# A two-layer transformer step on one core: even and odd heads of the first mixer in turn on the upper and lower rows of the matmul array, small products placed among long ones, and the first experts' rows gathered between their first weight blocks

## The chip, the core and the metric

The kernel runs on one core of a Trainium2 chip. A core has TensorE (PE; its weight loads are listed as PEld), VectorE (DVE), ScalarE (ACT), GpSimd (POOL) and a queue engine (SP) that issues the DMAs here. The metric is the device time of one execution in microseconds; the time of the kernel before is the median of three runs.

## The reference, cut to what matters

The program computes a first block and then two layers of a second one, for 256 tokens of width 1024. The change lies in the first block alone. Its mixer has a gated linear attention (GLA) with 4 heads (key width 64, value width 128, both directions, chunks of 64 tokens) and a Hyena branch (two long convolutions); after it come a router and 16 experts that take 32 tokens each.

```python
def _gla_direction(q, k, v, la, s0, with_output):
    kc, vc, lac = _chunk(k), _chunk(v), _chunk(la)
    b = jnp.cumsum(lac, axis=3)
    b_last = b[:, :, :, -1]
    upd = jnp.einsum('bhncd,bhnce->bhnde', kc * jnp.exp(b_last[:, :, :, None] - b), vc)
    ...
    scores = jnp.einsum('bhncd,bhnsd->bhncs', qc * jnp.exp(b - ref), kc * jnp.exp(ref - b))
    ...
    o = (jnp.einsum('bhncs,bhnse->bhnce', scores, vc)
         + jnp.einsum('bhncd,bhnde->bhnce', qc * jnp.exp(b), s_prev))

def _hyena(hp, conv_w, conv_b, filt, bias):
    u = _short_conv(hp, conv_w, conv_b)
    v, x1, x2 = jnp.split(u, 3, axis=-1)
    z = x1 * _bidir_fftconv(v, filt[0, 0], filt[0, 1], bias[0])
    return x2 * _bidir_fftconv(z, filt[1, 0], filt[1, 1], bias[1])

def _ec_moe(h, w_router, w_gate, w_up, w_down):
    ...
    vals, idx = lax.top_k(jnp.swapaxes(aff, 1, 2), cap)
    xs = h[bidx, idx]
    hid = jax.nn.silu(jnp.einsum('becd,edf->becf', xs, w_gate)) * jnp.einsum('becd,edf->becf', xs, w_up)
```

## The kernel before

Each engine runs its own list of instructions, and semaphores join them. For the first mixer the list is a table of steps, `MIX1`: a setup, then four strands (projections and Hyena; GLA of direction 0; GLA of direction 1 with its output; late blocks of the `ada` weights) that `merged` deals out by the cost in `COST` and the share of each strand. The table `AFTER` holds a step back until another has been dealt. All engines walk through `MIX1` in the same order, each doing its own part of a step. So the order of PE, DVE and ACT in the mixer comes from this one table.

The steps that matter here, by the names in the code and the lines of the profile:

- `st(d, s)` (L845), the chunk updates of direction `d` for context (`s` = 1) or latents (0): 16 products with 64 contracted rows and 64 columns of weights. Two loops, the outer one over `odd`, which decides the half of the 128 rows.
- `scr(d, e)` (L855), the scores inside chunks: for the even heads (`e` = 0, rows 0 to 63) and then the odd ones (rows 64 to 127) 4 products each.
- `o_(e)` (L872 and L876), the output of the even and then of the odd heads: products of all 128 rows (values by scores) and of 64 rows (state by queries), four groups of 2 and 4 instructions in a call.
- `osum` (L885): sums of squares of the output, 8 products with one column. ACT squares first (L2675). `ob` turns the result round (L640).
- `ht` (L672), `sp` (L683), `hy` (L635), `ut` (L640), `cv` (L748), `ic` (L635): Hyena's filters, their spectra, its projections (12, in three weight blocks), the transpose before a transform, the transform, and the way back. `sp` and `cv` take four PSUM banks in a row. DVE multiplies the spectra between `cv` and `ic` (L1720 to L1739).
- `ada` (L700): 8 steps with one weight block each, whose sum `mod(1)` (L713) spreads.
- `out` (L635) and `rows`: the output projection, its transposes and the router's products; then softmax (ACT L2731), top 32 of each expert (DVE L1904 to L1913) and a gather of tokens by a product with a 0/1 matrix, `slots(x)` (L635, 16 instructions), in front of the products of experts 4x to 4x+3, `four_experts` (L959).

One product in float32 shows as two matmul records in the trace.

All weights come as blocks of up to 2 MB through a ring of places in SBUF in a fixed order on SP's queue. A block's DMA is issued when the block that had its place before has been read. In the mixer three places are in use; the others lie over the mixer's own buffers. They open when those are done: the first of them waits for `ic(1, 3)`, the next ones also for `o`, and one for the last `out`. Ten blocks fit before the first experts' block must have been read.

```python
                if block_before(i) is not None:
                    q.wait_ge(*at("read", block_before(i)))
                if i == SLOTS.index(4):
                    q.wait_ge(*at("ic", 1, 3))
                if SLOTS[i] in (YE_SLOT, XS_SLOT, HM_SLOT):
                    q.wait_ge(*at("full", "o", 1))
```

Of the kernel before, what the change touches and what calls it, by code (L numbers as in the profile page):

```python
# [117 lines left out]
AFTER = {("hy", 0): ("sp", 1), ("b", 1, 1): ("v", 1, 1), ("o", 0): ("scr", 0, 1)}  # L118
# [265 lines left out]
def rows64(e):  # L384
    return slice(64 * e, 64 * e + 64)
# [5 lines left out]
def program(nc, ring_d, ranked_d, p1_d, p2_d, pf_d, xT_d, cT_d, pos_d, out_d):  # L391
    order, slot_read = [], []
    with contextlib.ExitStack() as ctx:
# [216 lines left out]
        def tensor(g):  # L610
# [224 lines left out]
            def st(d, s):  # L835

                g.wait_ge(*at("kt", d, s))
                g.wait_ge(*at("v", s, 1))
                for odd in range(2):
                    ps, r = fresh("st", d, s, odd), rows64(odd)  # L840
                    for ti in range(2):
                        for hp in range(2):
                            for e in range(2):
                                hd, c = 2 * hp + e, ti * 256 + hp * 128
                                ins = g.matmul(ps[rows64(e), c:c + 128], KT[d][r, ti, hd * 64:(hd + 1) * 64],  # L845
                                               vT[s][r, ti, hd * 128:(hd + 1) * 128], start=True, stop=True)
                    ins.then_inc(*full("st", d, s, odd))

            def scr(d, e):
                r = rows64(e)  # L850
                ps = fresh("scr", d, e)
                g.wait_ge(*at("k2", d))
                for hp in range(2):
                    for ti in range(2):
                        ins = g.matmul(ps[:, (hp * 2 + ti) * 128:(hp * 2 + ti + 1) * 128], KT[d][r, hp, ti * 128:(ti + 1) * 128],  # L855
                                       K1[d][r, hp, ti * 128:(ti + 1) * 128], start=True, stop=True)
                ins.then_inc(*full("scr", d, e))

            def o_(e):
                ps = fresh("o", e)  # L860
# [5 lines left out]
                for hp in range(2):  # L866
                    hd = 2 * hp + e
                    hv, r = slice(hd * 128, (hd + 1) * 128), rows64(e)
                    for ti in range(2):
                        c0 = hp * 256 + ti * 128  # L870
                        for d in range(2):
                            g.matmul(ps[:, c0:c0 + 128], vT[0][:, ti, hv], SCR[d][:, e, hp, ti, :], start=d == 0, stop=False)  # L872
                        for n in (2 * ti, 2 * ti + 1):
                            for d in range(2):
                                o0 = c0 + 64 * (n % 2)
                                ins = g.matmul(ps[:, o0:o0 + 64], SP[r, d, n, hp, :], Q2[d][r, hp, 64 * n:64 * n + 64],  # L876
                                               start=False, stop=n % 2 == 1 and d == 1)
                ins.then_inc(*full("o", e))
# [23 lines left out]
            def out_(b):  # L902
# [46 lines left out]
            def four_experts(ps, key, done, rows_of, ready=None):  # L949

                for part in range(4):
                    w, i = weights(*key, part)
                    wv = w.rearrange("p k (e n) -> p k e n", e=4) if len(w.shape) == 3 else w.rearrange("p (k e n) -> p k e n", k=2, e=4)
                    if ready:
                        g.wait_ge(*at(*ready, part // 2))
# [15 lines left out]
            def slots(x):  # L971
# [3 lines left out]
                g.wait_ge(*at("pm", x > 0))  # L975
                for q in range(2):
# [5 lines left out]
                    ins.then_inc(*full("xs", x, q))  # L982

# [17 lines left out]
            slots(0)  # L1001
# [18 lines left out]
            for x in range(4):  # L1020
                for half in range(2):
                    for mat in range(2):
                        ps = fresh("gu", x, half, mat)
                        four_experts(ps, (("w_gate", "w_up")[mat], x, half), ("gu", x, half, mat),
                                     lambda kk, e: XS[x][:, kk, 32 * e:32 * e + 32], ("xs", x))
# [551 lines left out]
        def vector(v):  # L1577
# [344 lines left out]

            def slots(x):
# [8 lines left out]
            slots(0)  # L1932
# [587 lines left out]
        def scalar(s):  # L2520
# [147 lines left out]
            def o_(e):  # L2668
                full("o", e)
                s.activation(OS.rearrange("p (h e) t -> p h e t", e=2)[:, :, e, :], bank("o", e).rearrange("p (h t) -> p h t", h=2), ACT.Copy) \  # L2670
                    .then_inc(*out("o", e))
# [27 lines left out]
            def normed(ti):  # L2699
                s.activation(HT[:, ti, :], HT[:, ti, :], ACT.Copy, bias=0.0, scale=RS1[:, ti:ti + 1]).then_inc(*out("hn", ti))  # L2700

# [24 lines left out]
            s.activation(STAT[:, 62:63], EPS5, ACT.Exp, bias=0.0, scale=1.0).then_inc(*out())  # L2726
# [3 lines left out]
            s.wait_ge(*at("lsub"))  # L2730
            s.activation(AE, AE, ACT.Exp, bias=0.0, scale=1.0).then_inc(*out("aexp"))  # L2731
            normed(1)
            slots(0)
# [656 lines left out]
```

## Time and profile before

| what | value |
|---|---|
| median of three runs | 1692.89 us (1688.23, 1694.29, 1692.89) |
| the profiled execution | 1685.1 us |
| its span in the trace | 1683.2 us |
| PE busy | 1423.9 us (85%) |
| PEld busy | 796.6 us (47%) |
| DVE busy | 509.1 us (30%) |
| ACT busy | 314.7 us (19%) |
| moved by DMA | 492.62 MB, mean 293 GB/s |
| granted clock of TensorE, mean | 0.921 of 2.4 GHz |

The span is the time between the first and the last record; 1.9 us of the execution lie around it. The shares are averages over stages with different limits: the first mixer ends at about 286 us, the first block's experts at about 745 us, and the two layers of the second block follow. A granted clock of 0.50 in a stretch is the lower of the two levels, 1.2 GHz, and 1.00 the upper one, 2.4 GHz.

### The profile page before, as it was taken

The numbers are of one execution on the slowest core, as the hardware profiler recorded it, in microseconds if no ns is written. First come the engines' busy times: TensorE is split into PE (matmuls) and PEld (weight loads), VectorE is DVE, ScalarE is ACT, GpSimd is POOL, SyncE is SP. The second block draws the span as 40 slices with busy tenths as digits, with TensorE's granted clock in tenths as the row PEclk, the third lists the DMA queues.
The fourth block names the chain that finished last, engine by engine and source line by source line (L and its number), as shares of the span: only waits on it lengthen the run. The fifth ranks groups of instructions, "written<-read, shape, count | busy, mean of one in ns | idle before, by whom it ended". The sixth has DMA issues, their size and how long they took to land.

```text
span 1683.2 us, 19028 instructions
## 1 busy us (share of the span) xinstructions
PE 1423.9 (85%) x7528; PEld 796.6 (47%) x7528; DVE 509.1 (30%) x1140; ACT 314.7 (19%) x659; POOL 0.2 (0%) x4
## 2 busy tenths in 40 slices
PE   6999998765766656579999899987899998999877
PEld 3665777321221211146768643432467677434323
DVE  5125362200111100014674422221336644222213
ACT  2422111100000000012322312210222223122102
POOL 0000000000000000000000000000000000000000
PEclk9999799888887878789999899999999999999989
DMA  9465219999999999991521389999715123799994
GB/s 383 167 228 200 100 50 390 382 428 428 427 428 428 428 428 427 426 415 53 200 100 51 150 338 412 412 417 411 322 50 200 64 87 150 311 415 408 416 413 161
DMA packets 56386, 492.62 MB, mean 293 GB/s; under 512 B 6240, under 2 KB 6624, under 8 KB 25952
## 3 DMA queue, kind: packets, MB, share of 16 engines
q1 hardware_dynamic: 56144, 491.15, 71.4%
q8 instruction: 66, 1.08, 0.3%
q14 instruction: 32, 0.26, 0.0%
q10 hardware_dynamic: 144, 0.13, 0.0%
HBM read 490.21 MB, written 1.05 MB: 292 GB/s over the span
## 4 chain that ended last, share of the span: by engine, by line
PE 60%; DMA 25%; DVE 6%; SPq 6%; issue 2%; ACT 1%; DVEq 0%; ACTq 0%
DMA A<-ring_d 21%; PE PS L635 20%; PE PS L1455 7%; SPq L3059 6%; PE PS L1484 4%; PE PS L959 4%; DMA A<-ranked_d 4%; PE PS L1319 3%; PE PS L640 3%; PE PS L1435 2%; PE PS L1501 2%; PE PS L1308 1%; PE PS L1145 1%; PE PS L1272 1%; PE PS L700 1%
## 5 line engine op out<-in xcount | busy, mean ns | idle before, releaser
L635 PE MATMUL PS<-A 128*128 128x256 f32 (+6 forms) x1720 | 413.7, 399 | 5.0 <-DMA A<-ring_d 2.7
L959 PE MATMUL PS<-A 128*32 128x512 f32 x1536 | 236.6, 753 | 143.4 <-DMA A<-ring_d 143.1
L635 PEld LDWEIGHTS PS<-A 128*128 128x128 f32 (+1 forms) x1720 | 308.5, 197 | 100.8 <-issue 58.4
L1455 PE MATMUL PS<-A 128*64 128x512 f32 (+1 forms) x1024 | 197.5, 635 | 23.7 <-DMA A<-ranked_d 23.6
L959 PEld LDWEIGHTS PS<-A 128*32 128x32 f32 x1536 | 52.2, 124 | 317.9 <-issue 239.7
L1455 PEld LDWEIGHTS PS<-A 128*64 128x64 f32 (+1 forms) x1024 | 58.5, 131 | 142.9 <-issue 141.0
L1975 DVE TENSOR_TENSOR A<-A,PS 128x512 f32<-128x512 f32 x8 | 5.5, 688 | 331.1 <-PE PS L959 331.1
L1484 PE MATMUL PS<-A 128*64 128x512 f32 (+1 forms) x512 | 94.9, 597 | 0.7 <-issue 0.7
L640 PE MATMUL PS<-A 128*128 128x128 f32 (+1 forms) x444 | 69.5, 289 | 29.2 <-DVE A L1975 7.1
L640 PEld LDWEIGHTS PS<-A 128*128 128x128 f32 (+1 forms) x444 | 53.5, 148 | 69.0 <-issue 39.2
L2426 DVE TENSOR_TENSOR A<-A,PS 128x256 f32<-128x256 f32 x26 | 11.0, 423 | 214.5 <-ACT A L2964 214.5
L1319 PE MATMUL PS<-A 128*128 128x256 f32 x256 | 58.3, 383 | 2.3 <-DVE A L2240 1.2
L1484 PEld LDWEIGHTS PS<-A 128*64 128x64 f32 (+1 forms) x512 | 27.1, 126 | 64.6 <-issue 63.3
L1501 PE MATMUL PS<-A 128*128 128x512 f32 x104 | 52.4, 628 | 5.2 <-issue 5.2
L1319 PEld LDWEIGHTS PS<-A 128*128 128x128 f32 x256 | 47.7, 190 | 10.5 <-issue 3.0
L2964 ACT ACTIVATE A<-PS 128x256 f32<-128x256 f32 x26 | 10.0, 386 | 224.9 <-PE PS L1455 224.9
L1435 PE MATMUL PS<-A 128*128 128x256 f32 (+1 forms) x256 | 49.3, 343 | 0.0
L2432 DVE COPY A<-PS 128x512 f32<-128x512 f32 x26 | 18.0, 692 | 102.0 <-PE PS L1484 102.0
L1435 PEld LDWEIGHTS PS<-A 128*128 128x128 f32 x256 | 41.0, 190 | 15.6 <-issue 12.0
L2069 DVE TENSOR_TENSOR A<-PS,A 128x512 f32<-128x512 f32 (+1 forms) x24 | 16.5, 688 | 63.2 <-PE PS L1145 63.2
L2878 ACT ACTIVATE A<-A 128x128 f32<-128x128 f32 (+1 forms) x48 | 21.2, 443 | 75.4 <-DVE A L2202 75.4
L2421 DVE TENSOR_SCALAR A<-PS,A 128x256 f32<-128x256 f32 (+1 forms) x64 | 28.6, 489 | 18.3 <-PE PS L1435 17.6
(352 smaller groups left out, 1259.6 us busy)
## 6 DMA issues: line engine op xcount, KB each, us to landing
A<-ring_d SPq DMA_DIRECT2D x156, 2048.0 KB, 23.3
A<-ranked_d SPq DMA_DIRECT2D x72, 1024.0 KB, 16.4
A<-ranked_d SPq DMA_DIRECT2D x144, 512.0 KB, 15.3
A<-ring_d SPq DMA_DIRECT2D x2, 1312.0 KB, 21.7
A<-ring_d SPq DMA_DIRECT2D x2, 1280.0 KB, 21.9
A<-p_d SPq DMA_DIRECT2D x1, 1232.0 KB, 21.9
A<-xT_d SPq DMA_DIRECT2D x1, 1024.0 KB, 5.6
A<-cT_d SPq DMA_DIRECT2D x1, 1024.0 KB, 12.0
```

The source lines that it names most:

```text
L635: ins = g.matmul(out, l, r, start=n == 0, stop=n == len(pairs) - 1)
L640: return g.transpose(out, in_, ident[0:k, 0:k])
L959: ins = g.matmul(ps[32 * e:32 * e + 32, :], rows_of(kk, e), wv[:, kk % 2, e, :], start=kk == 0, stop=kk == 7)
L1319: ins = g.matmul(bank("wo", l, b)[:, j * 256:(j + 1) * 256], w[:, k, c:c + 128], O[:, k, :], start=k == 0 and j == 0, stop=k == 7, skip_gr ...
L1435: ins = g.matmul(ps[:, c:c + w], XGT[:, x, d * 128:(d + 1) * 128], px, start=True, stop=True)
L1455: ins = g.matmul(ps[m * s:m * s + m, :], XS2[u % 2][:, kk, c:c + m], wv[:, kk % nk, s, :], start=kk == 0, stop=kk == 7)
L1484: ins = g.matmul(ps[m * s:m * s + m, :], HD[n % 2][:, f, m * s:m * s + m], wd[f][:, s, half * 512:(half + 1) * 512], start=f == 0, stop=f ...
L1501: ins = g.matmul(PS[:, b, :], QT[p % 2], YE2[p % 2][:, half * 512:(half + 1) * 512], start=n == 0, stop=last)
L2421: ins = v.tensor_scalar(XS2[u % 2][:, d, 0:w], bank("xs2", l, u, part, 1)[:, j * 256:j * 256 + w], gain, bias, ALU.mult, ALU.add)
L2432: v.tensor_copy(YE2[p % 2][:, 512:1024], bank("ye2", l, p, 1)).then_inc(*out("ye2", l, p, 1))
L2878: ins = s.activation(p, p, ACT.Exp, bias=ST[:, i, c:c + 1], scale=1.0, accum_out=ST[:, i, 4 + c:5 + c])
L3059: q.dma_start(RING[x][:, s * n:(s + 1) * n], src).then_inc(*land(f"ring{x}", *(("landed", i) if s == len(of) - 1 else ())))
```

## The change

The change does four things.

1. In `st`, `scr` and `o_` the loop over the two halves of the rows becomes the inner one, so that products on rows 0 to 63 and rows 64 to 127 follow each other, into two PSUM banks. `scr(d, 0)` does both halves and `scr(d, 1)` nothing on PE. `o_(hp)` now does one pair of heads, even and odd, and keeps both banks from the first call to the second; ACT copies both after the second.
2. Eight entries of `AFTER` instead of three, of which these change the order:

```diff
-AFTER = {("hy", 0): ("sp", 1), ("b", 1, 1): ("v", 1, 1), ("o", 0): ("scr", 0, 1)}
+AFTER = {("hy", 0): ("sp", 1), ("b", 1, 1): ("v", 1, 1), ("o", 0): ("hy", 3), ("o", 1): ("cv", 0), ("osum",): ("hy", 7), ("ob", 0): ("ic", 0, 3),
+         ("mod", 1): ("ic", 0, 3), ("sp", 0): ("ada", 9), ("sp", 1): ("ada", 10)}
```

3. The first `out` product no longer waits for `ic(1, 3)` as a whole: the first seven of its eight parts wait for `ic(1, 2)`, the last for `ic(1, 3)`. On ACT the load of the exponential's table and the softmax's exponential move ahead of the last copy of `rows` and of both `normed` steps.
4. The gather for experts 0 to 3 is cut in four, `first_slots(q)`: two parts stand ahead of the first weight block of `w_gate`, the third ahead of the second block and the fourth ahead of the third. Each block waits for its own part alone. ACT takes over parts 0 and 2 from PSUM and DVE parts 1 and 3.

```diff
             def st(d, s):
+                ps = [fresh("st", d, s, odd) for odd in range(2)]
                 g.wait_ge(*at("kt", d, s))
                 g.wait_ge(*at("v", s, 1))
-                for odd in range(2):
-                    ps, r = fresh("st", d, s, odd), rows64(odd)
-                    for ti in range(2):
-                        for hp in range(2):
-                            for e in range(2):
+                for ti in range(2):
+                    for hp in range(2):
+                        for e in range(2):
+                            for odd in range(2):
...
             def scr(d, e):
-                r = rows64(e)
-                ps = fresh("scr", d, e)
+                if e:
+                    return
+                ps = [fresh("scr", d, x) for x in range(2)]
                 g.wait_ge(*at("k2", d))
                 for hp in range(2):
                     for ti in range(2):
+                        for x in range(2):
+                            r = rows64(x)
+                            ins = g.matmul(ps[x][:, (hp * 2 + ti) * 128:(hp * 2 + ti + 1) * 128], KT[d][r, hp, ti * 128:(ti + 1) * 128],
+                                           K1[d][r, hp, ti * 128:(ti + 1) * 128], start=True, stop=True)
...
+            def o_(hp):
+                for x in range(2):
+                    if hp == 0:
+                        fresh("o", x, hold=True)
+                ps = [bank("o", x) for x in range(2)]
...
+                for ti in range(2):
+                    c0 = hp * 256 + ti * 128
+                    for x in range(2):
+                        hd = 2 * hp + x
                         for d in range(2):
+                            g.matmul(ps[x][:, c0:c0 + 128], vT[0][:, ti, hd * 128:(hd + 1) * 128], SCR[d][:, x, hp, ti, :], start=d == 0, stop=False)
+                    for n in (2 * ti, 2 * ti + 1):
+                        for d in range(2):
+                            o0 = c0 + 64 * (n % 2)
+                            for x in range(2):
+                                r = rows64(x)
+                                ins = g.matmul(ps[x][:, o0:o0 + 64], SP[r, d, n, hp, :], Q2[d][r, hp, 64 * n:64 * n + 64],
                                                start=False, stop=n % 2 == 1 and d == 1)
...
                 g.wait_ge(*at("mix", 1))
-                g.wait_ge(*at("ic", 1, 3))
-                for j in range(2):
-                    c = (b % 2) * 256 + j * 128
-                    ins = group(ps[:, j * 256:(j + 1) * 256], [(hold["outw"][:, k, c:c + 128], T[:, k, :]) for k in range(8)])
+                for k0, k1 in ((0, 7), (7, 8)) if b == 0 else ((0, 8),):
+                    g.wait_ge(*at("ic", 1, k1 - 5))
...
                 for part in range(4):
+                    for q in ahead[part]:
+                        first_slots(q)
                     w, i = weights(*key, part)
...
+            def first_slots(q):
+                g.wait_ge(*at("hn", 0))
+                g.wait_ge(*at("hn", 1))
+                g.wait_ge(*at("pm", False))
+                ps = fresh("xs", 0, q)
+                for j in range(2):
+                    c = (2 * q + j) * 128
+                    ins = group(ps[:, j * 128:(j + 1) * 128], [(HT[:, ti, c:c + 128], places_of(ti, 0, 4).rearrange("p e j -> p (e j)"))
+                                                               for ti in range(2)])
+                ins.then_inc(*full("xs", 0, q))
...
+                                     ((), (), (), ()) if x or half or mat else ((0, 1), (2,), (3,), ()))
...
                     s.activation(MS1, MS1, ACT.Sqrt, bias=EPS6, scale=1.0).then_inc(*out("hstd"))
+                    s.activation(STAT[:, 63:64], EPS5, ACT.Exp, bias=0.0, scale=1.0).then_inc(*out())
+                    s.wait_ge(*at("lsub"))
+                    s.activation(AE, AE, ACT.Exp, bias=0.0, scale=1.0).then_inc(*out("aexp"))
```

**PE around the filters' spectra.** L672 is `ht`, L855 `scr`, L845 `st`, L683 `sp`, L700 `ada`, L635 `hy`. Before:

```order
L672 MATMUL PS<-A 128x512 x5
L855 MATMUL PS<-A 128x128 x4
L672 MATMUL PS<-A 128x512
L845 MATMUL PS<-A 64x128 x16
L672 MATMUL PS<-A 128x512
L855 MATMUL PS<-A 128x128 x4
L672 MATMUL PS<-A 128x512
L683 MATMUL PS<-A 128x512 x4
L700 MATMUL PS<-A 32x512 x8
L683 MATMUL PS<-A 128x512 x4
L635 MATMUL PS<-A 128x256 x16
```

After, with the lines of the changed kernel (`ht` L673, `scr` L862, `st` L847, `sp` L684, `ada` L701, `hy` L636):

```order
L673 MATMUL PS<-A 128x512 x5
L862 MATMUL PS<-A 128x128 x8
L673 MATMUL PS<-A 128x512
L847 MATMUL PS<-A 64x128 x16
L673 MATMUL PS<-A 128x512 x2
L701 MATMUL PS<-A 32x512 x8
L684 MATMUL PS<-A 128x512 x4
L701 MATMUL PS<-A 32x512 x8
L684 MATMUL PS<-A 128x512 x4
L862 MATMUL PS<-A 128x128 x8
L636 MATMUL PS<-A 128x256 x24
```

An `ada` step has moved in front of the first `sp`, another stands between the two, and the scores of direction 1 follow the second `sp` in one piece.

**PE around the output of GLA and the first transform.** L635 is `hy`, L855 `scr`, L872 and L876 `o_`, L640 `ut`, L748 `cv`, L700 `ada`. Before:

```order
L700 MATMUL PS<-A 32x512 x8
L635 MATMUL PS<-A 128x256 x8
L855 MATMUL PS<-A 128x128 x4
L635 MATMUL PS<-A 128x256 x8
L855 MATMUL PS<-A 128x128 x4
L872 MATMUL PS<-A 128x128 x2
L876 MATMUL PS<-A 128x64 x4
...
L640 MATMUL PS<-A 128x128 x8
L748 MATMUL PS<-A 128x512 x4
L700 MATMUL PS<-A 32x512 x8
L872 MATMUL PS<-A 128x128 x2
```

After (`hy` L636, `o_` L883 and L889, `ut` L641, `cv` L749, `osum` L900):

```order
L701 MATMUL PS<-A 32x512 x8
L636 MATMUL PS<-A 128x256 x8
L883 MATMUL PS<-A 128x128 x4
L889 MATMUL PS<-A 128x64 x8
...
L641 MATMUL PS<-A 128x128 x8
L749 MATMUL PS<-A 128x512 x4
L883 MATMUL PS<-A 128x128 x4
L889 MATMUL PS<-A 128x64 x8
...
L636 MATMUL PS<-A 128x256 x32
L900 MATMUL PS<-A 128x1 x8
```

The output's first half now follows the whole of `hy(3)` with nothing of `scr` between them, its second half follows `cv(0)` directly, and all four of the next `hy` stand ahead of `osum`. In each half the groups are twice as long and half as many.

**PE at the first experts.** L640 is the last transpose of the routing, L635 the gather, L959 the experts' products. Before:

```order
L640 MATMUL PS<-A 128x16 x2
L635 MATMUL PS<-A 128x128 x16
L959 MATMUL PS<-A 32x512 x64
L640 MATMUL PS<-A 128x128 x4
L635 MATMUL PS<-A 128x36 x8
```

After (L641, L636 and L980):

```order
L641 MATMUL PS<-A 128x16 x2
L636 MATMUL PS<-A 128x128 x8
L980 MATMUL PS<-A 32x512 x8
L636 MATMUL PS<-A 128x128 x4
L980 MATMUL PS<-A 32x512 x8
L636 MATMUL PS<-A 128x128 x4
L980 MATMUL PS<-A 32x512 x48
```

The first block of eight products stands behind 8 instead of 16 instructions of the gather.

## Rows read from the trace of the kernel before

**Rows 1.** DMA and engines by stretch: length, busy times, clock, DMA share, GB/s.

```profile
257.00:304.00 47.00, 35.22 (x187) 31.39 (x187) 14.07 (x46) 6.36 (x10) 0.00 (x0) 0.86 1.00 426
304.00:314.00 10.00, 10.00 (x94) 4.50 (x97) 1.37 (x4) 3.39 (x6) 0.00 (x0) 0.98 0.66 245
340.00:740.00 400.00, 251.86 (x1552) 82.48 (x1553) 32.78 (x82) 24.38 (x48) 0.00 (x0) 0.81 1.01 428
```

**Rows 2.** SP's waits from 250 to 300 us, and its first issue after 300 us.

```profile
SPq L3100 <- DVE A L1837: 32.5, 1, 32.5
...
L3100 SPq DMA_DIRECT2D A<-ring_d x1: 336/336/336, 308.1 to 308.1; - x1
DMA to landing us min/median/max: 9.0/9.0/9.0
```

**Rows 3.** DVE from the end of cv(1) to ic(1, 3), first and last instruction.

```profile
234.67 1.22 DVE L1720 TENSOR_TENSOR A<-PS,A 128x1024 f32<-128x1024 f32 x1 [7.51 <-PE PS L748]
...
254.67 0.28 DVE L1837 TENSOR_TENSOR A<-A 128x128 f32<-128x128 f32 x1
```

**Rows 4.** The chain that ended last: start, length, work. Small products of the mixer.

```profile
99.06 1.52 PE PS L845 x32
...
133.34 1.09 PE PS L855 x8
...
192.34 0.64 PE PS L872 x4
192.98 1.03 PE PS L876 x8
```

**Rows 5.** The same chain: the two stretches from ut to the end of cv.

```profile
182.67 1.92 PE PS L640 x8
...
185.35 5.13 PE PS L748 x8
...
229.28 5.36 PE PS L748 x8
```

**Rows 6.** PE in order of time: start, length, work, idle before and its releaser.

```profile
141.35 3.67 PE L683 MATMUL PS<-A 128*128 128x512 f32 x8 [1.16 <-DVE A L1644]
...
170.81 0.82 PE L872 MATMUL PS<-A 128*128 128x128 f32 x4 [1.39 <-DVE A L1817]
...
204.57 2.83 PE L885 MATMUL PS<-A 128*128 128x1 f32 x16 [1.90 <-ACT A L2675]
...
227.30 1.20 PE L640 MATMUL PS<-A 128*128 128x128 f32 x8 [1.67 <-DVE A L1747]
```

**Rows 7.** Busy times and granted clock by stretch around o_(0) and behind osum.

```profile
170.80:188.00 17.20, 16.41 (x59) 13.18 (x60) 0.00 (x0) 1.79 (x3) 0.00 (x0) 0.51 0.24 104
206.00:208.00 2.00, 2.00 (x9) 1.91 (x10) 0.20 (x1) 0.27 (x1) 0.00 (x0) 0.50 0.00 0
```

**Rows 8.** PE in the second block: score products on one row half (first), on both (second).

```profile
862.30 0.93 PE L1270 MATMUL PS<-A 64*128 64x128 f32 x6
863.07 1.46 PE L1272 MATMUL PS<-A 64*128 64x256 f32 x6
...
874.26 0.49 PE L1270 MATMUL PS<-A 64*128 64x128 f32 x4
874.58 0.60 PE L1272 MATMUL PS<-A 64*128 64x256 f32 x4
```

**Rows 9.** ACT in order of time: last copy of rows, table load, normed(0), the exponential.

```profile
288.96 0.58 ACT L2688 ACTIVATE A<-PS 128x512 f32<-128x512 f32 x1
289.55 1.28 ACT L2726 ACT_TABLE_LOAD   x1
...
291.14 1.15 ACT L2700 ACTIVATE A<-A 128x1024 f32<-128x1024 f32 x1
292.20 0.21 ACT L2731 ACTIVATE A<-A 128x32 f32<-128x32 f32 x1
```

**Rows 10.** PE in order of time: the gather for the first experts.

```profile
300.64 5.58 PE L635 MATMUL PS<-A 128*128 128x128 f32 x32 [1.01 <-DVE A L1919]
```

More of the change, by code:

```diff
@@ L909, in out_ @@
                 g.wait_ge(*at("mix", 1))
-                g.wait_ge(*at("ic", 1, 3))
-                for j in range(2):
-                    c = (b % 2) * 256 + j * 128
-                    ins = group(ps[:, j * 256:(j + 1) * 256], [(hold["outw"][:, k, c:c + 128], T[:, k, :]) for k in range(8)])
+                for k0, k1 in ((0, 7), (7, 8)) if b == 0 else ((0, 8),):
+                    g.wait_ge(*at("ic", 1, k1 - 5))
+                    for j in range(2):
+                        c = (b % 2) * 256 + j * 128
+                        for k in range(k0, k1):
+                            ins = g.matmul(ps[:, j * 256:(j + 1) * 256], hold["outw"][:, k, c:c + 128], T[:, k, :],
+                                           start=k == 0 and j == 0, stop=k == 7, skip_group_check=True)
                 ins.then_inc(*full("out", b))
@@ L954, in four_experts @@
                     if ready:
-                        g.wait_ge(*at(*ready, part // 2))
+                        g.wait_ge(*at(*ready, part // 2 if ready[1] else part))
                     arrived(i)
@@ L1921, in places, with first_slots @@
                 ins.then_inc(*out(*key))
+            def first_slots():
+                for q in (1, 3):
+                    full("xs", 0, q)
+                    for j in range(2):
+                        d = 2 * q + j
+                        ins = v.tensor_scalar(XS[0][:, d, :], bank("xs", 0, q)[:, j * 128:(j + 1) * 128], MA[:, 4, d:d + 1],
+                                              MA[:, 5, d:d + 1], ALU.mult, ALU.add)
+                    ins.then_inc(*out("xs", 0, q))
             def slots(x):
@@ L2666, in qk, with o_ @@
                 s.activation(Q2[d], BB[d], ACT.Exp, bias=0.0, scale=1.0).then_inc(*out("q2", d))
[L2668 to L2671, printed above, removed]
+            def o_(hp):
+                if hp == 0:
+                    return
+                for e in range(2):
+                    full("o", e)
+                    s.activation(OS.rearrange("p (h e) t -> p h e t", e=2)[:, :, e, :], bank("o", e).rearrange("p (h t) -> p h t", h=2), ACT.Copy) \
+                        .then_inc(*out("o", e))
             def osum():
@@ L2700, in normed, with first_slots @@
                 s.activation(HT[:, ti, :], HT[:, ti, :], ACT.Copy, bias=0.0, scale=RS1[:, ti:ti + 1]).then_inc(*out("hn", ti))
+            def first_slots():
+                for q in (0, 2):
+                    full("xs", 0, q)
+                    for j in range(2):
+                        d = 2 * q + j
+                        ins = s.activation(XS[0][:, d, :], bank("xs", 0, q)[:, j * 128:(j + 1) * 128], ACT.Identity,
+                                           bias=MA[:, 5, d:d + 1], scale=MA[:, 4, d:d + 1])
+                    ins.then_inc(*out("xs", 0, q))
             def slots(x):
@@ L2729, in scalar @@
             normed(0)
-            s.wait_ge(*at("lsub"))
-            s.activation(AE, AE, ACT.Exp, bias=0.0, scale=1.0).then_inc(*out("aexp"))
             normed(1)
-            slots(0)
+            first_slots()
             for x in range(4):
```

39 lines of the change are left out of this document (14 added, 25 removed).

## The prediction

> **What bounds the kernel now.** I read the DMA by stretch first. From 257 to 304 us the weights flow at 426 GB/s, from 304 to 314 at 245, from 340 to 740 at 428 again, while PE works for only 252 of those 400 us [rows 1]. So the first block's experts are bound by their weights, and their end stands at a fixed distance from the start of that flow. What matters is when the flow starts and whether it has a hole. Its start is in SP's waits: the longest, 32.5 us, ends with DVE's L1837, in the step of `ic(1, 3)`, which opens the fourth place of the ring [rows 2]. That instruction closes 20.0 us of DVE's work without a gap, from 234.67 to 254.67, which starts when PE ends `cv(1)` [rows 3]. So the flow starts 20.0 us after `cv(1)`, and this distance isn't touched. The hole follows from the ring: ten blocks fit, then SP waits until the first experts' block has been read, issues at 308.1, and that block lands 9.0 us later [rows 2]. Its price is 10 us at 245 instead of 428 GB/s, 4.3 us [rows 1].
>
> Ahead of `cv(1)` PE is busy but for three places, which the waits in order of time show: 1.16, 1.39 and 1.67 us for DVE, and besides these 1.90 us for ACT [rows 6]. The granted clock tells the rest. It is 0.51 over the 17.2 us behind the wait of 1.39, the lower level nearly throughout, and 0.50 behind `osum` [rows 7].
>
> Behind the first experts nothing is changed, so I carry the shift to the end at its full size.
>
> **The change part by part.** First the shift of `cv(1)`'s end.
>
> *Row halves in turn.* The nearest rows are the score products of the second block. On one row half 6 records take 0.77 us from start to start, 128 ns each; on both halves in turn 4 take 0.32, 80 ns each; the longer form falls from 1.46/6 = 243 ns to 0.60/4 = 150 [rows 8]. Both ratios are 0.62. `scr` takes 1.09 a call, `o_`'s part of 64 rows 1.03 a group of eight records at the upper clock, `st` 1.52 [rows 4]. With 0.62, four `scr` save 4 x 0.41 = 1.65 us and eight groups of `o_` 8 x 0.39 = 3.1 us. The 128-row part of `o_` keeps its 0.64. `st` already takes only 1.52/32 = 48 ns a record, since its column halves are in turn; I take a third instead of 0.38, 0.5 us for each of four calls, 2.0 us. Bounds: nothing for all three (if the halves don't overlap), and half of each, 2.2 + 4.1 + 3.0 = 9.3 us instead of 6.75.
>
> The Trainium skill, TensorEngine Tiling (Array Packing), section Theoretical Speedup, gives up to 2x for a small dimension of 64 or less; by it these three would save the 9.3 us. The rows on the score products stop at 0.62, and I go by them.
>
> *Waits.* An `ada` step in front of the first `sp` takes 1.86 us (from 190.48, the end of `cv(0)`, to 192.34 [rows 4, 5]) and covers the 1.16 us for DVE. What is late next there is DVE's own list, but it ends its last `ht` about when PE ends that step, so I count the whole 1.16. The 1.39 us before `o_(0)` were for the masks of `scr(1, 1)`; these scores now lie three `hy` and an `ada` earlier: gone. The 1.67 us before `ut(1, 0)` are for DVE's `ic(0, 3)`; `ob` and `mod(1)` now stand between: gone. Sum 4.2 us, bounds 2 and 4.2. The 1.90 us before `osum` stay: ACT squares at its own place in the list, now behind `hy(7)` instead of `hy(4)`, so PE waits for one copy and the square exactly as now. I count nothing.
>
> *Clock.* The 17.2 us at the lower level began with the 1.39 us of idle time. Without it I expect the upper level there. `o_(0)` took 182.67 - 170.81 = 11.86 us; at the upper one the same work takes 4 x (0.64 + 1.03) = 6.68 [rows 4 to 6], 5.2 less. `ut(0)` with its wait took 2.68, `ut(1)` 1.98: 0.7 less. `cv(0)` took 5.13 against 3.67 for `sp`, which has the same form: 1.4 less [rows 5, 6]. Sum 7.3. `cv(1)` took 5.36 behind the wait of 1.67 [rows 5, 6]; without that wait 3.67, 1.7 less. Behind `osum` the wait stays, and I leave the lower clock with it. Sum 9.0 us. Bounds: nothing (if the small products hold the clock down by themselves), and 9.0 + 3 (if `osum`, too, keeps the upper level).
>
> *Sum of the mixer.* 6.75 + 4.2 + 9.0 = 19.9 us: `cv(1)`, and with it the start of the flow, comes 19.9 us earlier. DMAs of the mixer: the blocks of `ada` steps 9, 10 and `hy` go through three places in nearly the same order, and PE waits for none of them in this stretch today. I count nothing; a late block would cost up to 9 us, the landing time above.
>
> *The hole.* It closes as far as the first experts' block is read earlier relative to the flow. On ACT the exponential no longer stands behind the last copy (0.58) and `normed(0)` (1.15) [rows 9]: about 1.6 earlier, and DVE's routing follows it directly. The gather of 16 instructions took 5.58 us; only half of it now stands ahead of the block: 2.8 earlier [rows 10]. But the block comes into the stretch in which PE has just been idle and the clock is low: its 1.86 us (the form of an `ada` step) become up to 3.5, 1.6 lost. Net 2.8 us of the 4.3; bounds 1.2 and 4.3. The split of `out` would add to this and I count it at nothing, since the hole isn't deeper. The two other parts of the gather hide behind the flow, as PE works 63% of it.
>
> *Total.* 19.9 + 2.8 = 22.7 us. The profiled execution took 1685.1 us (span 1683.2), so it would take 1662.4. The median of the three runs is 1692.9, 7.8 above it; I take the same gain from that: **1670 us**. Three runs that lie 6 us apart can hardly tell less than 0.5%, 8.5 us, from no change.
>
> **The rivals.**
>
> *The clock falls at `o_(0)` anyway.* The output's first half and `ut` are small products for 6 us, and then PE waits for ACT's copy. For it: `o_(0)` stayed at the lower level to its end, though PE was busy for 16.4 of the 17.2 us [rows 7]. Against: `o_(1)`, the same products, ran at 0.64 and 1.03 all through [rows 4]. It takes back the 7.3: 1677 us. Chance 0.22.
>
> *The halves don't overlap in `st`, `scr` and `o_`,* since their weights, not their columns, take the time. Against it stand the score products, whose weights are as wide. It takes 6.75: 1677 us. Chance 0.10.
>
> *`osum` keeps the upper clock and the halves come nearer to 2x.* 3 + 2.5 + 1.5 for the hole: 1663 us. Chance 0.10.
>
> *The flow doesn't follow the mixer.* If another condition sets the issue of the first blocks, or a late `ada` or `hy` block takes the place of PE's waits, only the hole and a few us are left: 1684 to 1690 us. SP's wait names L1837 alone. Chance 0.08.
>
> *Slower: each switch between row halves empties the array.* A product then costs its whole way through the array. No row shows that price; the longer score product's pitch on one half, 243 ns [rows 8], is the nearest for a small product that isn't overlapped. At 0.24 us a record instead of 0.048 in `st` (128 records), 0.136 in `scr` (32) and 0.129 in `o_` (64), that is 25 + 3 + 7 = 35 us more than today; against the remaining gain of 16 us the kernel would be 19 us slower: 1712 us. It decides from 0.11 us more a record: 224 x 0.11 = 25 us eats the 16 and the measurement's 8.5. The pitch of 80 ns on alternating halves speaks against it. Chance 0.04.
>
> The Trainium skill, TensorEngine Tiling (Array Packing), section Key Properties, says that a change of the tiling mode, not of the tile, drains TensorE; by that rule halves in turn cost no drain, and the longer groups of `o_` halve its changes between 128 and 64 rows, a gain.
>
> **How the numbers follow.** My own case has 0.46, and between 1665 and 1675 us. The rivals to the fast side reach 1663, the two middle ones 1677, together 1679 to 1683 if both come. The range 1661 to 1682 leaves out some 2 in 10: the flow that doesn't follow, the slow rival, and the tails. Faster by over 0.5% (below 1684.4): 0.46 + 0.22 + 0.10 + 0.10 and a little of the fourth rival, 0.89. Within 0.5%: 0.07. Slower: 0.04.
>
> **What would show it.** PE's waits before `sp(0)`, `o_(0)` and `ut(1, 0)` gone, that before `osum` still near 1.9. Granted clock 1.00 from `o_(0)` to `cv(0)`, and `cv` at 3.7 us twice. Groups of 16 records in `o_` near 1.3 us instead of 2 x 1.03. SP's long wait ends near 235 us, again 20 us behind `cv(1)`. From 50 us behind it the DMA rate dips less than to 245 GB/s over ten us. PE's last expert product of the first block comes 23 us earlier, and no more is lost or won behind it. The prediction fails if PE's idle time only moves, if the clock falls again at a thin stretch, or if a wait for a DMA appears in the mixer.

## The result, and the profile after

The changed kernel takes 1662.36 us (median of 4 runs, 1661.39 to 1666.04); the kernel before, beside it, 1690.56 us (4 runs). The ratio is 0.9851, 95% interval 0.9821 to 0.988. In a second series it took 1662.15 us (6 runs, 1659.62 to 1666.87) against 1687.19, ratio 0.9858 (0.9835 to 0.988). Forecast were 1670 us and a range of 1661 to 1682.

The head of the page of the changed kernel, and its group of the first experts' products:

```profile
span 1659.6 us, 19035 instructions
...
PE 1409.5 (85%) x7528; PEld 781.9 (47%) x7528; DVE 509.7 (31%) x1140; ACT 314.5 (19%) x659; POOL 0.2 (0%) x4
...
L980 PE MATMUL PS<-A 128*32 128x512 f32 x1536 | 242.5, 769 | 138.2 <-DMA A<-ring_d 137.8
```

The span is 23.6 us shorter, and the experts' products still wait for the ring's blocks. The chain that ended last, from the changed kernel's scores to the DVE work behind `cv(1)` (start, length, work; L862 is `scr`, L883 and L889 `o_`, L641 `ut`, L749 `cv`, L636 `hy`):

```profile
132.99 1.09 PE PS L862 x16
...
167.55 0.89 PE PS L883 x8
168.44 1.04 PE PS L889 x16
...
171.61 0.69 PE PS L641 x4
...
173.55 3.67 PE PS L749 x8
...
181.33 0.59 ACT A L2716
...
182.05 14.07 PE PS L636 x64
...
208.71 3.69 PE PS L749 x8
212.42 1.24 DVE A L1754
```

Sixteen records of the scores take as long as eight did in [rows 4], and so do sixteen of the 64-row part of `o_`: 1.04 against 1.03. The eight records of the 128-row part take 0.89, and 1.09 in the second group of a call, where twice four took 1.28. Both `cv` take 3.7 us, against 5.13 and 5.36 in [rows 5]. `cv(1)` ends at 212.40 instead of 234.64, 22.2 us earlier. This trace had also started worse. The same `ada` step, ahead of the first instruction that was edited, before and after:

```profile
68.01 1.92 PE L700 MATMUL PS<-A 128*32 128x512 f32 x16
```

```profile
69.13 1.93 PE L701 MATMUL PS<-A 128*32 128x512 f32 x16
```

It is 1.1 us late there; from 20 to 40 us the granted clock was 0.81 against 0.95. Counted from this step, `cv(1)` moved by 23.4 us. PE's waits from the filters' spectra to `osum`, in order of time:

```profile
140.56 3.67 PE L684 MATMUL PS<-A 128*128 128x512 f32 x8 [0.61 <-DVE A L1678]
...
182.05 14.05 PE L636 MATMUL PS<-A 128*128 128x256 f32 x64 [0.77 <-ACT A L2716]
198.00 1.92 PE L900 MATMUL PS<-A 128*128 128x1 f32 x16 [1.90 <-ACT A L2721]
```

Of the waits in [rows 6] the second and the last are gone, the first has shrunk to 0.61, the one for ACT's square is where it was, and one is new: `hy(4)` waits 0.77 us for ACT's copy of `o_`. Engines and clock by stretch (columns as in [rows 7]) around `o_(0)` to `cv(0)`, behind `osum`, and over 65.5 us from the start of the weight flow; under it the same stretch of the kernel before.

```profile
167.40:177.00 9.60, 8.81 (x65) 6.42 (x64) 0.97 (x2) 2.67 (x4) 0.00 (x0) 1.00 0.86 365
198.00:206.00 8.00, 8.00 (x58) 8.00 (x58) 3.53 (x9) 1.42 (x2) 0.00 (x0) 0.79 0.56 231
232.50:298.00 65.50, 54.55 (x340) 38.90 (x339) 16.43 (x53) 9.85 (x16) 0.00 (x0) 0.90 0.99 410
```

```profile
254.70:320.00 65.30, 53.40 (x340) 39.45 (x340) 15.69 (x52) 9.75 (x16) 0.00 (x0) 0.90 0.94 389
```

The clock is at its upper level, 2.4 GHz, from `o_(0)` to `cv(0)`, and for part of the time behind `osum` at the lower one. The flow moves 410 GB/s on average instead of 389: against the full 428 that leaves 2.8 us of hole instead of 5.9 (65.5 x 18/428, 65.3 x 39/428). Of either, 1.7 us lie in the first 49 us, which flow at 413 GB/s. SP's wait for `ic(1, 3)`, and its first issue behind the ten blocks, as in [rows 2]; then PE at the gather and the first block, as in [rows 10]:

```profile
SPq L3155 <- DVE A L1871: 36.3, 1, 36.3
...
L3155 SPq DMA_DIRECT2D A<-ring_d x1: 337/337/337, 282.6 to 282.6; - x1
...
DMA to landing us min/median/max: 9.2/9.2/9.2
```

```profile
268.39 0.59 PE L641 MATMUL PS<-A 128*16 128x128 f32 x2 [3.57 <-DVE A L1932]
...
275.82 3.75 PE L636 MATMUL PS<-A 128*128 128x128 f32 x16 [1.01 <-DVE A L1953]
279.50 3.00 PE L980 MATMUL PS<-A 128*32 128x512 f32 x16
```

The issue came 25.5 us earlier (308.1 to 282.6), 3.3 us more than the flow's start. The first block took 3.00 us in place of 1.9, at the lower clock, and half the gather took 3.75.

Behind the first block the distance between the two traces isn't constant. First row of PE's products of the second block, and the last row of PE, before and after:

```profile
752.14 17.43 PE L635 MATMUL PS<-A 128*128 128x256 f32 x80
...
1675.28 2.58 PE L640 MATMUL PS<-A 128*128 128x128 f32 x16 [3.14 <-ACT A L2786]
```

```profile
724.05 17.43 PE L636 MATMUL PS<-A 128*128 128x256 f32 x80
...
1650.80 3.43 PE L641 MATMUL PS<-A 128*128 128x128 f32 x16 [3.15 <-ACT A L2841]
```

28.1 us at the start of the second block, 24.5 at the last transposes, which then take 0.85 us longer. At the last sums of squares of the first block it was 26.7 (741.87 and 715.20). I come back to this.

### The profile page after: what moved, and what is told of

Read it like the earlier page. It is cut to its first block, busy times and chain, and to the rows that moved or that the text cites. A ratio compares the mean times of both kernels' runs of the same rounds, so it can differ in the third digit from the quotient of the medians.

```text
span 1659.6 us, 19035 instructions
## 1 busy us (share of the span) xinstructions
PE 1409.5 (85%) x7528; PEld 781.9 (47%) x7528; DVE 509.7 (31%) x1140; ACT 314.5 (19%) x659; POOL 0.2 (0%) x4
## 4 chain that ended last, share of the span: by engine, by line
PE 61%; DMA 25%; DVE 5%; SPq 5%; issue 2%; ACT 1%; DVEq 0%; ACTq 0%
DMA A<-ring_d 21%; PE PS L636 19%; PE PS L1489 8%; SPq L3114 5%; PE PS L1518 4%; PE PS L980 4%; DMA A<-ranked_d 4%; PE PS L1353 3%; PE PS L641 3%; PE PS L1469 3%; PE PS L1535 2%; PE PS L930 2%; PE PS L1342 1%; PE PS L1179 1%; PE PS L1306 1%
## 5 line engine op out<-in xcount | busy, mean ns | idle before, releaser
L636 PE MATMUL PS<-A 128*128 128x256 f32 (+6 forms) x1592 | 383.1, 398 | 4.5 <-DMA A<-ring_d 2.6
L980 PE MATMUL PS<-A 128*32 128x512 f32 x1536 | 242.5, 769 | 138.2 <-DMA A<-ring_d 137.8
L636 PEld LDWEIGHTS PS<-A 128*128 128x128 f32 (+1 forms) x1592 | 283.0, 196 | 97.8 <-issue 60.0
L980 PEld LDWEIGHTS PS<-A 128*32 128x32 f32 x1536 | 53.0, 126 | 316.1 <-issue 244.6
L641 PE MATMUL PS<-A 128*128 128x128 f32 (+1 forms) x444 | 69.3, 289 | 25.9 <-DVE A L2018 7.1
L641 PEld LDWEIGHTS PS<-A 128*128 128x128 f32 (+1 forms) x444 | 54.1, 150 | 64.8 <-issue 32.9
## 6 DMA issues: line engine op xcount, KB each, us to landing
A<-ring_d SPq DMA_DIRECT2D x156, 2048.0 KB, 23.4
```

The costliest lines, as they stand in the source:

```text
L636: ins = g.matmul(out, l, r, start=n == 0, stop=n == len(pairs) - 1)
L641: return g.transpose(out, in_, ident[0:k, 0:k])
L980: ins = g.matmul(ps[32 * e:32 * e + 32, :], rows_of(kk, e), wv[:, kk % 2, e, :], start=kk == 0, stop=kk == 7)
```

## The experiments

My theory: the mixer's end sets the start of the flow, and it moved by three parts, idle time with the slow clock behind it, row halves that overlap, and, behind it, the hole. Rivals: small products hold the clock down by themselves; the halves gain only by fewer changes of the array; the end of the mixer isn't what binds. Times are medians; "before" is the kernel before on the same chip, 1690.13 us (17 runs) for e1 to e4 and 1687.19 us (11 runs) for the rest. The changed kernel itself was not timed beside e1 to e4, so e2 and e4 are set against its ten runs in the two other series, 1659.6 to 1666.9 us.

**e1, the order alone.** The kernel before with the new table.

```diff
-AFTER = {("hy", 0): ("sp", 1), ("b", 1, 1): ("v", 1, 1), ("o", 0): ("scr", 0, 1)}
+AFTER = {("hy", 0): ("sp", 1), ("b", 1, 1): ("v", 1, 1), ("o", 0): ("hy", 3), ("o", 1): ("cv", 0), ("osum",): ("hy", 7), ("ob", 0): ("ic", 0, 3),
+         ("mod", 1): ("ic", 0, 3), ("sp", 0): ("ada", 9), ("sp", 1): ("ada", 10)}
```

> The kernel before with the new table AFTER alone: the order of the mixer's steps, no row halves in turn, no change to out, softmax or the first gather. Theory (the wait ahead of o(0) brings the clock down, and the order removes it): the end of cv(1) comes 13 to 15 us earlier than 234.64, granted clock 1.00 from o(0) to cv(0), time 14 us below the kernel before. Rival (small products of 64 rows one half at a time hold the clock down by themselves, and only the halves in turn keep it up): clock 0.50 from o(0) to cv(0) as before, gain 4 to 6 us.

1676.46 us (6 runs), ratio 0.9937 (0.9913 to 0.9961). PE in order of time at `o_(0)` and `cv(0)` (L873, L877, L749), and the clock over that stretch:

```profile
169.99 0.61 PE L873 MATMUL PS<-A 128*128 128x128 f32 x4
170.53 1.10 PE L877 MATMUL PS<-A 64*128 64x64 f32 x8
...
178.59 3.67 PE L749 MATMUL PS<-A 128*128 128x512 f32 x8 [0.79 <-ACT A L2609]
```

```profile
170.00:182.10 12.10, 11.31 (x65) 8.49 (x64) 0.97 (x2) 3.27 (x5) 0.00 (x0) 1.00 0.69 292
```

No wait stands before `o_(0)`, and the clock is 1.00 although the halves still come one after the other. `cv(1)` ended 14 us earlier (217.01 + 3.67 = 220.7). The rival that needs the halves for the clock falls. The median moved by 13.7 us, the ratio of all runs by 11 (7 to 15).

**e2, the halves apart.** The changed kernel, the loop over halves outermost in `st` and `scr`, and in `o_`:

```diff
-                    for n in (2 * ti, 2 * ti + 1):
-                        for d in range(2):
-                            o0 = c0 + 64 * (n % 2)
-                            for x in range(2):
+                    for x in range(2):
+                        for n in (2 * ti, 2 * ti + 1):
+                            for d in range(2):
+                                o0 = c0 + 64 * (n % 2)
```

> The changed kernel with the two row halves one after the other again inside each group of st, scr and o_; groups, banks and order stay. Theory (the halves overlap): a group of 16 records of o_ takes 2.06 us instead of 1.04, scr 2.2 instead of 1.1, st 1.54 instead of 1.04; 4 + 2 + 2 us, so 8 us slower than the changed kernel. Rival (the gain came from fewer changes between 128 and 64 rows): within 1 us of the changed kernel.

1670.62 us (6 runs), ratio 0.9888 (0.9868 to 0.9907): 8 us above the changed kernel by the medians, as forecast, and 5 to 6 by the ratios; all six runs, from 1667.35, lie above its ten. But the rows aren't those of the forecast. The chain of e2:

```profile
138.10 1.64 PE PS L862 x16
140.79 1.55 PE PS L847 x32
...
174.19 0.89 PE PS L883 x8
175.08 1.53 PE PS L889 x16
```

A group of 16 in `o_` takes 1.53, between the 2.06 of two groups of eight before and the 1.04 of halves in turn; `scr` takes 1.64, between 2.18 and 1.09. So both theories hold a half: joining two groups took off 0.5 us, putting the halves in turn another 0.5. `st` had its groups joined before, and takes 1.55 as then. In this trace the halves apart account for 4 x 0.5 + 2 x 0.55 + 4 x 0.5 = 5.1 us. `cv(1)` ended 9.7 us later than in the trace of the changed kernel (222.1 against 212.4), and the rest of this isn't theirs: e2's trace was 3.6 us late by 72 us already, ahead of the first instruction that was edited, where the same products ran at a lower clock and one wait for a DMA was 0.9 us longer, and behind `osum` the lower clock cost 1.6 us more.

**e3, the tail alone.** The changed kernel with the mixer of before; what stays are the split `out`, the early exponential and the gather in parts.

```diff
-AFTER = {("hy", 0): ("sp", 1), ("b", 1, 1): ("v", 1, 1), ("o", 0): ("hy", 3), ("o", 1): ("cv", 0), ("osum",): ("hy", 7), ("ob", 0): ("ic", 0, 3),
-         ("mod", 1): ("ic", 0, 3), ("sp", 0): ("ada", 9), ("sp", 1): ("ada", 10)}
+AFTER = {("hy", 0): ("sp", 1), ("b", 1, 1): ("v", 1, 1), ("o", 0): ("scr", 0, 1)}
...
-                ps = [fresh("st", d, s, odd) for odd in range(2)]
```

> The changed kernel with the mixer's table, st, scr and o_ of before: only the split out, the early exponential and the gather in four parts are left. Theory (the hole in the weight flow closes by about 3 us): the flow starts at 254.7 as before, time 3 us below the kernel before. Rival (the earlier gather only makes PE wait for the flow): no difference.

1683.04 us (12 runs, 1674.24 to 1689.65), ratio 0.997 (0.9953 to 0.9987), so 5 us (2 to 8) below before by the ratio and 7 by the medians, where I expected 3. Its profiled run is the fastest of the twelve, and shows what I hadn't expected. PE in order of time at `o_(0)` (L872, L876) and `cv(0)` (L748), and the clock:

```profile
170.30 0.68 PE L872 MATMUL PS<-A 128*128 128x128 f32 x4 [1.39 <-DVE A L1836]
170.91 1.10 PE L876 MATMUL PS<-A 64*128 64x64 f32 x8
...
178.97 3.67 PE L748 MATMUL PS<-A 128*128 128x512 f32 x8 [0.79 <-ACT A L2636]
```

```profile
170.30:188.00 17.70, 16.91 (x106) 11.99 (x107) 5.21 (x6) 3.30 (x5) 0.00 (x0) 1.00 0.38 143
```

The mixer is that of before, the wait of 1.39 us is there, and the clock stays at 1.00. In [rows 7] the same stretch was at 0.51. So the wait doesn't always bring the clock down, and what a fall costs can be read off two traces of one mixer: `cv(1)` ended 8 us earlier here (226.8 against 234.64), 7.3 of them from the end of the wait to the end of `cv(0)` (190.48 - 170.81 = 19.7 against 182.64 - 170.30 = 12.3).

How often the fall comes, the times tell roughly. My estimate for the profiled execution of before without it is 1685.1 - 7.3 = 1677.8 us. The fastest of the 32 timed runs of before took 1682.9, and of the twelve of e3 only the profiled one is under 1680. So it is likely the rule in this order of steps, and its absence the exception; no other run's trace shows it.

**e4, the wait put back.** The changed kernel with `scr(1)` directly ahead of `o_(0)`.

```diff
-("o", 0): ("hy", 3), ("o", 1): ("cv", 0)
+("scr", 1, 0): ("hy", 3), ("o", 0): ("hy", 3), ("ut", 0, 0): ("o", 0), ("o", 1): ("cv", 0)
```

> The changed kernel with scr(1) directly ahead of o(0), behind hy(3), so that o(0) waits for DVE's masks again. Theory (that wait brings the clock down): a wait of 1 to 2 us, then 0.50 granted until cv(0) is half through; 1.5 us of wait and 5 to 6 us of slow clock, 7 us slower than the changed kernel. Rival (a wait costs only itself): 1.5 us slower.

1670.17 us (6 runs), ratio 0.9883 (0.986 to 0.9905), 8 us above the changed kernel by the medians and 4 to 5 by the ratios; five of the six runs lie above its ten. PE in order of time:

```profile
170.20 1.13 PE L883 MATMUL PS<-A 128*128 128x128 f32 x8 [1.99 <-DVE A L1851]
171.25 1.24 PE L889 MATMUL PS<-A 64*128 64x64 f32 x16
172.42 2.07 PE L883 MATMUL PS<-A 128*128 128x128 f32 x8
174.43 1.97 PE L889 MATMUL PS<-A 64*128 64x64 f32 x16
...
179.09 5.28 PE L749 MATMUL PS<-A 128*128 128x512 f32 x8 [0.78 <-ACT A L2651]
```

The wait is 1.99 us, and 2 us behind its end the products take twice as long, until `cv(0)` is half through. From the start of `o_(0)` to the end of `cv(0)` it is 14.2 us instead of 9.8, so the slow clock cost 4.3 us, less than the 5 to 6 expected. `cv(1)` ends 8.8 us later than in the changed kernel; the rest is the wait, another of 0.81 us for ACT ahead of `hy(3)` that the edit brought, and 1.6 us more of slow clock behind `osum`. A wait that costs only itself is refuted for this run.

**a1, the changed kernel again.** No edit.

> The changed kernel itself, to have its time on the same chip as the three others: 1662 us if the chip is like the first, its end of cv(1) within 1 us of 212.4.

1662.15 us, the figures above; `cv(1)` ended at 212.3.

**e7, the gather in one piece.**

```diff
-                    for q in ahead[part]:
-                        first_slots(q)
...
             ins.then_inc(*full("post"))
+            slots(0)
```

(In the kernel the list `ahead` is emptied, and ACT and DVE call `slots(0)` too.)

> The changed kernel with the gather for experts 0 to 3 in one piece again (16 instructions ahead of the first block). Theory (the gather's half ahead of the first block sets when the ring's fourth place is free, and so the hole in the flow): the first block is read 1.5 to 2.8 us later, the rate over the ten us around it falls, time 2 us above the changed kernel. Rival (the hole was closed by the earlier exponential alone): no difference.

1665.24 us (6 runs), ratio 0.9866 (0.9846 to 0.9886), against 0.9858 (0.9835 to 0.988) for a1: the medians are 3.1 us apart, the intervals overlap. Its flow by stretch, 65.3 us from its start:

```profile
234.60:299.90 65.30, 54.34 (x353) 40.36 (x352) 16.47 (x54) 10.34 (x17) 0.00 (x0) 0.90 0.97 404
```

404 GB/s lie between the 410 of the changed kernel and the 389 of before: a hole of 3.7 us against 2.8 and 5.9. So in these traces the gather in parts closes 0.9 us of the hole, and the other 2.2 of the 3.1 come from the exponential and the split of `out`. I had given the gather 2.8 - 1.6 = 1.2, and the exponential 1.6.

The 0.9 depends on the clock at the first block. In the changed kernel and a1 it took 3.00 and 2.93 us; in e2, e3, e4, e8 and e9, with the same gather, 1.92 to 1.98, and there such a stretch flowed at 415 or 416 GB/s. Against those the parts close 1.7 to 1.8 us. By time alone the gain of the gather isn't shown: the trace of e7 is 2.3 us late at the end of `cv(1)`, where nothing was edited.

**e8, longer groups in `o_`.** All the 128-row products of a call first, then its 64-row ones.

```diff
                         for d in range(2):
-                            g.matmul(ps[x][:, c0:c0 + 128], vT[0][:, ti, hd * 128:(hd + 1) * 128], SCR[d][:, x, hp, ti, :], start=d == 0, stop=False)
+                            g.matmul(ps[x][:, c0:c0 + 128], vT[0][:, ti, hd * 128:(hd + 1) * 128], SCR[d][:, x, hp, ti, :],
+                                     start=d == 0 and ti == 0, stop=False, skip_group_check=True)
+                for ti in range(2):
+                    c0 = hp * 256 + ti * 128
```

> The changed kernel with the two groups of each call of o_ joined: 8 products of 128 rows, then 16 of 64 rows, so that the array changes between the two half as often. Theory (each change costs some tenths of a us, which is why eight 128-row records took 1.0 instead of 1.28 in the changed kernel): 0.2 to 0.3 us less in each call, 0.5 us in all, not to be told from the changed kernel by time. Rival (no cost in a change): the same length of a call, 4.2 us.

1662.71 us (6 runs), ratio 0.9864 (0.9841 to 0.9886): not to be told from a1. PE in order of time, `o_(0)` whole, then `ut`:

```profile
167.39 1.95 PE L883 MATMUL PS<-A 128*128 128x128 f32 x16
169.26 2.00 PE L892 MATMUL PS<-A 64*128 64x64 f32 x32
171.20 1.23 PE L641 MATMUL PS<-A 128*128 128x128 f32 x8
```

A call takes 3.81 us (171.20 - 167.39) where it took 4.15 in a1 (171.43 - 167.28). Two changes between 128 and 64 rows fewer save 0.34 us, 0.17 each.

**e9, what is left of the waits.** e8, ACT's square right behind its copies, and the banks of `o` held until `hy(4)` has its own:

```diff
+                settle()
+                s.activation(OQ, OS, ACT.Square, bias=0.0, scale=1.0).then_inc(*out("oq"))
 
             def osum():
-                settle()
-                s.activation(OQ, OS, ACT.Square, bias=0.0, scale=1.0).then_inc(*out("oq"))
...
+                if m == 4:
+                    banks.release("o", 0)
+                    banks.release("o", 1)
```

> The changed kernel with three further edits: ACT squares the output of GLA right behind its two copies instead of behind hy(7); the two banks of o are released only when hy(4) has its bank, so that hy(4) doesn't wait for ACT's copies; the groups of e8. Theory: the 1.90 us ahead of osum and the 0.77 us ahead of hy(4) go, the clock stays up behind osum (1.6 us), and with 0.5 us of the groups cv(1) ends 4 to 5 us earlier, time 1658 us. Rival (another wait takes their place, as osum's result is needed no earlier): less than 1.5 us.

1659.34 us (6 runs, 1657.02 to 1666.09), ratio 0.9842 (0.9818 to 0.9866). PE in order of time (L636 `hy`, L905 `osum`, L752 `cv(1)`), and the clock:

```profile
179.52 14.08 PE L636 MATMUL PS<-A 128*128 128x256 f32 x64
193.44 1.84 PE L905 MATMUL PS<-A 128*128 128x1 f32 x16
...
203.05 3.67 PE L752 MATMUL PS<-A 128*128 128x512 f32 x8 [1.39 <-DVE A L1702]
```

```profile
193.00:207.00 14.00, 12.61 (x86) 10.43 (x85) 8.13 (x21) 4.22 (x6) 0.00 (x0) 1.00 0.41 152
```

Both waits are gone and the clock stays up behind `osum`; `cv(1)` waits 1.39 instead of 0.79, now for DVE, and ends 5.6 us earlier than in a1 (206.7 against 212.3), of which 0.9 was there at `o_(0)` already, ahead of the first edit (166.38 against 167.28). No fall of the clock follows this wait of 1.39 us either. The median is 2.8 us below a1's, but the intervals of the ratios overlap, so by time alone it isn't shown to be faster than the changed kernel.

## Why the prediction was right

Its frame held: the flow of weights starts 20 us behind `cv(1)` (232.44 - 212.42 = 20.0 again), and the first block's end moves with the flow. e1 shows it from the other side, with the mixer alone 14 us shorter. The sum for the mixer was 19.9 us, measured 22.2, or 23.4 counted from 68 us. Term by term, from the two traces:

| term | forecast | measured |
|---|---|---|
| `st` | 2.0 | 1.9 (four times 1.52 to 1.04) |
| `scr` | 1.65 | 2.2 (two pairs, 2.18 to 1.09) |
| `o_`, 64 rows | 3.1 | 4.1 (four pairs, 2.06 to 1.04) |
| `o_`, 128 rows | 0 | 1.2 (5.12 to 3.96) |
| waits | 4.2 | 2.8 (0.55, 1.39 and 1.67 gone, 0.77 new) |
| clock, `o_(0)` to `cv(0)` | 7.3 | 7.3 (11.86, 2.68, 5.13 to the upper level's times) |
| clock at `cv(1)` | 1.7 | 1.7 |
| clock around `osum` | 0 | about 1.8 (in these two traces) |
| hole | 2.8 | 3.1 |

The measured column adds to 23.0 for the mixer, 0.4 short of the 23.4. The 1.8 around `osum` is partly luck: e1, e2, e4 and e7 have the same steps from `osum` on, and in them the lower clock lasted longer, so that the way from `osum` to the transposes behind took 8.7 us against 7.1 in the changed kernel, a1 and e8.

*Where it was off.* The step "Both ratios are 0.62" was mis-sized for `scr` and `o_`: against before the measured ratio is 0.5. The 0.62 came from rows of the second block in which groups of 6 and of 4 records are compared, so that nothing was joined, and in e2 the halves in turn alone give 1.04/1.53 = 0.68 and 1.09/1.64 = 0.66, close to it; the rest is the joining, which I hadn't priced, although the order rows showed it. Here the bound of up to 2x for 64 rows came out nearer, which the Trainium skill gives (TensorEngine Tiling (Array Packing), section Theoretical Speedup) and which the prediction set against its rows, but half of it for a reason that the section doesn't name. The 128-row part gained by it as well. By e8 a change between 128 and 64 rows costs 0.17 us; the Trainium skill says in the section Key Properties of that page that a change of the mode drains TensorE, and gives no figure.

*The waits.* The sum "I count the whole 1.16" was wrong by half: DVE's own list was late, as the text said it might be, and 0.61 remained. The new wait of 0.77 had no term: both banks of `o_` are freed by ACT only after the second call, and `hy(4)` takes the first of them. That is a wait in the place of another, small enough.

*The clock.* Its size was right. Its cause was put too simply. "The 17.2 us at the lower level began with the 1.39 us of idle time" is what the trace shows; that without the wait the clock stays up was borne out in e1 and the changed kernel, and e4 brought the fall back with the wait. But e3 shows the wait without the fall, and in e9 a wait as long before `cv(1)` had none behind it. So the change takes away the occasion of a fall that cost 7.3 us, which by the times came in most runs with this order of steps and in one trace was absent. The rival "the clock falls at `o_(0)` anyway" came in none of the seven traces that have that order and no wait there (the changed kernel twice, e1, e2, e7, e8, e9).

*The hole.* 3.1 us by the rates, close to the 2.8. Inside it the gather was worth 0.9, not 1.2, and `out` and the exponential 2.2. Both terms of the gather were too large. The half ahead of the block took 3.7 us (279.50 - 275.82), since it is the half at the lower clock (granted 0.50 there), where the whole took 5.5 in e7 (283.57 - 278.04): 1.8 saved, not 2.8. The block at the lower clock took 3.0 us, which gave back 1.1, not 1.6. "The split of `out` would add to this and I count it at nothing" left out a term: DVE's last addition for `out` (L1844 before, L1878 after) comes 0.9 us earlier relative to the flow, and the softmax's sums (L1894, L1928) 1.7 more, which is the exponential's 1.6. Neither was run apart.

*The rivals.* The fast one, halves near 2x and the upper clock behind `osum`, had 1663 us and a chance of 0.10. Its first half came, its second for a part of the stretch, and the kernel lies at its figure: the likeliest case named the right mechanisms and took `scr`, `o_` and the clock behind `osum` too small. The two middle rivals together would give 1670 + 7.3 + 6.75 = 1684 us, not 1679 to 1683; nothing hangs on it, as neither came.

*The time.* From the profiled execution the forecast was 1662.4 us, measured 1661.5. From the median it was 1670, measured 1662.4: the gain is 28.2 us by the medians (25.0 beside a1) where 22.7 were forecast, so the time lies near the fast end of the range. That the two profiled executions differ by 23.6, close to the 22.7, is in part luck: behind the first block, in code that wasn't changed, the distance shrank from 26.7 us to 23.6, where the prediction said that no more would be lost or won. The same products at the end of the first layer, before and after:

```profile
1203.30 1.97 PE L1110 MATMUL PS<-A 128*128 128x256 f32 x8 [0.73 <-ACT A L2985]
```

```profile
1175.07 3.75 PE L1144 MATMUL PS<-A 128*128 128x256 f32 x8 [0.73 <-ACT A L3040]
```

The distance falls by 2.1 us around them, and by 4.1 at the end of the second layer, the 0.85 of the last row among them; between, some of it comes back. It isn't the change that costs this: e1 and e3, with other mixers, also take 3.75 at the first place, and all nine other traces take 2.0 to 3.9 us longer than that of before from the end of the first block on. The profiled execution of before lies 7.8 us under the median of its three runs, that of the changed kernel 0.9 under its own. So to take the gain from one profile and subtract it from the median hid some 3 us of it.

*What stays open.* The last sums of squares of the first block come 26.7 us earlier, 1.4 more than mixer and hole give (22.2 + 3.1); where the 1.4 arise in 400 us of flow I haven't traced. The other 1.4 of the 28.1 are the clock at the first products behind it (L1131 took 6.50 us, L1165 5.15), which the change doesn't touch. Why the clock falls behind the same wait in one run and not in another no run shows.

## What to carry to other kernels

Where one stream of weights bounds the second half of a stage, look for what opens it: here one DVE instruction 20 us behind one product, and every microsecond of PE ahead of that product counted in full. Look beyond one profile of each kernel: the trace of before ran faster than any of nine others in code that they share, and so hid part of the gain. Read idle time together with the granted clock behind it: 1.4 us of waiting cost a further 7.3 us by slow products behind it in one trace and nothing in another, so a wait of this size is worth removing even where it looks small, and one profile doesn't tell its mean price. Products on 64 rows should come in long groups and with the halves in turn: in `scr` and `o_` each of the two gave about half of the gain.

## What the runs showed of the hardware

- The granted clock can be at either level behind the same wait in the same instruction stream: 0.51 over the 17.2 us behind 1.39 us of idle time in one trace, 1.00 in another (before, e3). At the lower level it stayed for 17 us while PE was busy for 16.4 of them with small products and a transform.
- In code that is the same in all ten traces, eight records took 1.97 us in four and 3.75 in six (L1110 before, L1144 after).
- Eight 64-row records (four products) with 128 columns of weights and 64 moving columns: 1.03 us in groups of 8 records (before), 0.77 for each eight when 16 of them stand together one half after the other (e2), 0.52 with the halves in turn (the changed kernel).
- A change between 128-row and 64-row products costs about 0.17 us (e8 against a1).
- Sixteen 128-row records in one run take 1.87 us, 117 ns each, against 160 ns in groups of four (e8, before).
